# Two transformer blocks on one core: two heads in each attention step, dense groups between the steps

## The reference, cut to what matters

```python
h = rms_norm(x, norm_w);  p = h @ w_in          # split into 18 parts
# A: sparse attention (DSA), 8 heads of 64, indexer of 4 heads
score = einsum('bth,bths->bts', iw, relu(einsum('bthd,bsd->bths', iq, ik)))   # causal
_, sel = top_k(score, 128)
p_a   = softmax(q_cat . kv_cat[sel]);  y_a = (p_a . c_kv[sel]) @ w_uv
# B: stick-breaking attention, 8 heads of 64
z = q k^T / 8;  log_stay = where(strict, log_sigmoid(-z), 0)
a = where(strict, exp(log_sigmoid(z) + cumsum_reverse(log_stay) - log_stay), 0);  y_b = a . v
# C: mLSTM, 4 heads of 128, gates i and f, causal convolution of width 4 + silu on q and k
h_c = num / max(|den|, exp(-m));  y_c = head_layer_norm(h_c) * sigmoid(ml_o)
branches = [y_a * silu(dsa_z), y_b * silu(sb_z), y_c * silu(ml_z)]
mixed = sum_k sigmoid(merge_k) * (branches_k @ w_branch_k);  x = x + mixed @ w_out
```

## Time and profile before

| | us |
|---|---|
| median of three runs | 3041.71 |
| profiled execution | 3063.43 |
| its span | 3061.7 |
| TensorE busy | 2803.4 (92%) |
| VectorE, ScalarE, POOL busy | 1198.1, 1052.6, 1249.1 |
| weight_low on POOL, 398 chunks | 959.1 |
| mean granted clock of TensorE | 0.943 |

### The profile page before, as it was taken

The page is one execution under the profiler, slowest core; times in us unless marked ns, Lnnn a source line. Parts: engine busy times, 40 slices in busy tenths (PEclk is TensorE's granted clock), DMA queues, the critical chain, the costliest instruction groups (busy, mean ns, idle before and its releaser), DMA issues.

```text
span 3061.7 us, 30072 instructions
## 1 busy us (share of the span) xinstructions
PE 2803.4 (92%) x12066; PEld 2149.4 (70%) x12066; DVE 1198.1 (39%) x1739; ACT 1052.6 (34%) x1591; POOL 1249.1 (41%) x803
## 2 busy tenths in 40 slices
PE   7999889989899988998998999997888889899997
PEld 5486667668666766766786887874466768788886
DVE  3652341433347125234323313168885543311112
ACT  3323453432332235443233333241215533332221
POOL 3133343334323333422443443457766334434442
PEclk9799999999989999989999999998788999999999
DMA  3131001122212210111222222231011112222222
GB/s 132 42 108 55 28 28 64 54 76 97 76 62 71 74 43 20 55 55 53 92 96 90 96 97 87 98 125 55 28 35 63 63 48 97 90 87 98 98 97 76
DMA packets 61510, 222.60 MB, mean 73 GB/s; under 512 B 7055, under 2 KB 8591, under 8 KB 60732
## 3 DMA queue, kind: packets, MB, share of 16 engines
q1 hardware_dynamic: 60556, 217.54, 21.0%
q0 software_dynamic: 816, 3.15, 0.3%
HBM read 218.52 MB, written 3.98 MB: 73 GB/s over the span
## 4 chain that ended last, share of the span: by engine, by line
PE 79%; DVE 10%; ACT 6%; POOL 3%; issue 2%; DMA 0%; SPq 0%; DVEq 0%; ACTq 0%
PE proj L154 67%; PE att L681 1%; PE proj L709 1%; DVE hT L432 1%; PE proj L796 1%; PE proj L735 1%; POOL probs L1225 1%; POOL weight_low L132 1%; PE att L726 1%; PE att L755 1%; DVE h_low L426 1%; DVE rstd L429 1%; PE att L700 1%; DVE turned L1115 1%; DVE probs L1137 1%
## 5 line engine op out<-in xcount | busy, mean ns | idle before, releaser
L132 POOL TENSOR_TENSOR weight_low<-ring,weight_high 128x1024 fp32r<-128x1024 f32 x398 | 959.1, 2411 | 1486.7 <-ACT weight_high L124 1486.5
L154 PE MATMUL proj<-h_high,weight_high 128*128 128x512 f32 x2096 | 843.8, 403 | 56.2 <-issue 19.2
L154 PE MATMUL proj<-h_high,weight_low 128*128 128x512 f32 x2096 | 831.8, 397 | 0.0
L154 PE MATMUL proj<-h_low,weight_high 128*128 128x512 f32 x2096 | 830.6, 396 | 0.0
L124 ACT ACTIVATE weight_high<-ring 128x1024 fp32r<-128x1024 f32 x398 | 419.1, 1053 | 488.6 <-PE proj L154 461.5
L154 PEld LDWEIGHTS proj<-h_high,weight_high 128*128 128x128 f32 x2096 | 403.0, 192 | 192.5 <-issue 46.1
L154 PEld LDWEIGHTS proj<-h_low,weight_high 128*128 128x128 f32 x2096 | 403.1, 192 | 87.2
L154 PEld LDWEIGHTS proj<-h_high,weight_low 128*128 128x128 f32 x2096 | 404.3, 193 | 82.1 <-issue 0.2
L2089 DVE TENSOR_TENSOR b_big<-proj,b_big 128x512 f32<-128x512 f32 x44 | 30.4, 691 | 395.6 <-PE proj L154 395.6
L154 PE MATMUL proj<-b_act_high,weight_high 128*128 128x512 f32 x352 | 138.5, 393 | 3.2 <-POOL weight_low L132 3.2
L154 PE MATMUL proj<-b_act_high,weight_low 128*128 128x512 f32 x352 | 138.0, 392 | 0.0
(11 more groups left out here) (391 smaller groups left out, 4211.3 us busy)
## 6 DMA issues: line engine op xcount, KB each, us to landing
ring<-in_stream SPq DMA_DIRECT2D x398, 512.0 KB, 3.2
xT<-in_x SPq DMA_DIRECT2D x2, 1024.0 KB, 6.1
out<-hT SPq DMA_DIRECT2D x1, 2048.0 KB, 6.3
consts<-in_const SPq DMA_DIRECT2D x1, 1088.0 KB, 10.7
bias_rows<-bias_row SPq DMA_DIRECT2D x2, 512.0 KB
b_logits<-in_mem POOLq DMA_DIRECT2D x1, 1024.0 KB, 7.3
bias_rows<-bias_row SPq DMA_DIRECT2D x1, 768.0 KB
raw<-in_wuk SPq DMA_DIRECT2D x2, 256.0 KB, 3.8
```

What stands on the lines that cost most here:

```text
L132: self.s_low.on(pool.tensor_tensor(self.low[:, c % self.slots, :], self.raw[:, c % self.slots, :], self.high[:, c % HIGH, :], ALU.subtract))
L154: mm = pe.matmul(out, a, b, start=(k == 0 and i == 0), stop=(k == n - 1 and i == 2))
```

## The change

In short: (a) Both attentions go through four steps of two heads instead of eight of one. Scores of the two heads alternate, one on array rows 0 to 63, the other on 64 to 127, into banks of their own; the value products alternate on the two column halves into one bank. Transposes and running sums are as many as before, head after head. (b) Dense groups are put between the steps, by the four tables below: the token groups sbv and two groups each of mlq and mlk ahead of the transposes, another behind them, and token groups mlv and all eight gate{d}0 groups around the running sums. The gates are copied out raw, and one sigmoid over 128x4096 is done ahead of the mLSTM heads; mlo and zc stand in those heads instead. Weight chunks come in the new order. (c) The indexer's scores go to attention banks, the largest block of queries first, with ReLU results in four places instead of two. (d) The single matmuls of the rotations, keys, values and gate transposes stand between dense groups, and their results are copied out by ScalarE; the key's and queries' turns, the gate rows and the latent's scaling on VectorE stand inside the 16 rounds of the search. (e) VectorE takes the mean over each head's channels from mv (`centre`), so num comes out centred, and the four mean groups of a layer go. The second head of a pair has soft_high in two tiles of its own.

```diff
+BEFORE_TURN = [[f"sbv{i}" for i in range(4)], [f"sbv{i}" for i in range(4, 8)], ["mlq2", "mlq3"], ["mlk1", "mlk2"]]
+AFTER_TURN = [["mlq0"], ["mlq1"], ["mlk0"], ["mlk3"]]
+BEFORE_SUMS = [[f"mlv{i}" for i in range(4)], ["gate10", "gate20"], [f"mlv{i}" for i in range(4, 8)], ["gate50", "gate60"]]
+AFTER_SUMS = [["gate00"], ["gate30"], ["gate40"], ["gate70"]]
...
+        g += [(n, "a") for n in BEFORE_TURN[p]]
+        g += [(n, "a") for n in AFTER_TURN[p]]
+        g += [(f"dsa{p}", "v")]
+    for p in range(PAIRS_H):
+        g += [(n, "a") for n in BEFORE_SUMS[p] + AFTER_SUMS[p]] + [(f"sb{p}", "v")]
+    g += [("mu0", "a"), ("mm0", "a")]
...
+        def index_scores(part):
+            for b, h in part:
+                r = slice(64 * (h % 2), 64 * (h % 2) + 64)
+                bank, col = (att[4 + h % 2], WQ[1] * (h // 2)) if b == 1 else (att[h], 0)
+                s_sc.on(pe.matmul(bank[:, col:col + WQ[b]], idx[r, h // 2, b * P:(b + 1) * P], idx[r, 2, 0:WQ[b]],
+                                  start=True, stop=True))
...
+        def dsa_scores(p):
+            if p == 0:
+                pe.wait_ge(s_rq.sem, s_rq.base + 4)
+                G.moved(pe, "kk3")
+                pe.wait_ge(s_relu.sem, s_relu.base + 12)
+            else:
+                pe.wait_ge(s_TA.sem, s_TA.base + 2 * p)
+                pe.wait_ge(s_TV.sem, s_TV.base + 4 * p)
+            for b in (3, 2, 0, 1):
                 bank, col = KPLACE[TB - 1 - b]
-                mm = pe.matmul(att[bank][:, col:col + WQ[b]], dq[r, h // 2, b * P:(b + 1) * P],
-                               dk[r, h // 2, 0:WQ[b]], start=True, stop=True)
+                for hh in range(2):
+                    mm = pe.matmul(att[2 * bank + hh][:, col:col + WQ[b]], dq[rows(hh), p, b * P:(b + 1) * P],
+                                   dk[rows(hh), p, 0:WQ[b]], start=True, stop=True)
...
+        def dsa_turn(p):
+            for hh in range(2):
+                pe.wait_ge(s_scaled.sem, s_scaled.base + 8 * p + 4 * (hh + 1))
+                for s in range(TB):
+                    bank, col = KPLACE[s]
+                    for b in range(s, TB):
+                        tr = pe.transpose(att[2 * bank + hh][:, col + (b - s) * P:col + (b - s + 1) * P],
+                                          probs[:, hh, OQ[b] + s * P:OQ[b] + (s + 1) * P], ident)
+                s_T.on(tr)
...
+        def pair_values(name, p, v):
+            out = G.open(pe, name)
+            for s in range(TB):
+                for hh in range(2):
+                    h = 2 * p + hh
+                    mm = pe.matmul(out[rows(hh), s * P:T], v[:, s, h * HD:(h + 1) * HD],
+                                   turned[:, hh, KOFF[s]:KOFF[s] + WK[s]], start=(s == 0), stop=(s == TB - 1),
+                                   skip_group_check=True)
...
+        dsa_scores(0)
+        for p in range(PAIRS_H):
+            fill(BEFORE_TURN[p])
+            dsa_turn(p)
+            fill(AFTER_TURN[p])
+            if p + 1 < PAIRS_H:
+                dsa_scores(p + 1)
+            else:
+                sb_scores(0)
+            dsa_values(p)
+        for p in range(PAIRS_H):
+            fill(BEFORE_SUMS[p])
+            sb_sums(p)
+            fill(AFTER_SUMS[p])
+            if p + 1 < PAIRS_H:
+                sb_scores(p + 1)
+            sb_values(p)
...
+        ml_rows(0)
+        ml_scores(0)
+        ml_scores(1)
+        for h in range(ML_H):
+            dense(f"mlo{h}")
             gated_product(2 * h, 0)
...
+        ml_rows(0)
+        G.moved(act, f"dsa{PAIRS_H - 1}")
+        for j in range(4):
+            s_zh.on(act.activation(z_high[0][:, j, :], za[:, j, :], ACT.Copy))
+        settle(act, s_a)
+        s_gate0.on(act.activation(mixed, mixed, ACT.Sigmoid))
+        for h in range(ML_H):
+            move(f"mlo{h}", mlo[:, h, :], ACT.Sigmoid)
+            W.round(act, f"proj{2 * h}0")
             move(f"den{h}", dn, ACT.Abs)
-            first_gate(2 * h + 1)
-            G.moved(act, f"mean{h}")
+            move(f"zc{h}", zc[:, h, :], ACT.Silu)
+            W.round(act, f"proj{2 * h + 1}0")
+            G.moved(act, f"num{h}")
             s_sq2.on(act.activation(hsq, hml, ACT.Square))
             move(f"var{h}", rstd[:], ACT.Sqrt, scale=1.0 / ML_D, bias=S.eps)
+            if h + 1 < ML_H:
+                ml_rows(h + 1)
         G.whole(act, f"num{ML_H - 1}")
...
+        for i in range(TOPK // 8):
             for b in range(1, TB):
                 x = score[:, OQ[b]:OQ[b] + WQ[b]]
                 link(dve.max(top8[:, b, :], x))
                 link(dve.match_replace(out=x, in_to_replace=top8[:, b, :], in_values=x, imm_value=TAKEN))
+            if i == 1:
+                latent()
+            if i == 4:
+                turn_key()
+            if i == 5:
+                gate_rows()
+            if 9 <= i <= 12:
+                turn_query(i - 9)
...
+            names = BEFORE_TURN[p]
+            for hh in range(2):
+                W.rest(pool, names[-1] if hh else names[len(names) // 2 - 1])
+                pool.wait_ge(s_rinv.sem, s_rinv.base + 2 * p + hh + 1)
+                for b in range(TB):
+                    x = probs[:, hh, OQ[b]:OQ[b] + WQ[b]]
+                    o = 24 + 4 * hh + b
+                    s_scaled.on(pool.tensor_scalar(x, x, small[:, o:o + 1], 1.0, ALU.mult, ALU.mult))
+            W.rest(pool, AFTER_TURN[p][-1])
...
+            names = BEFORE_SUMS[p]
+            softplus(p, 0)
+            fill(names[0:len(names) // 4])
+            softplus(p, 1)
+            fill(names[len(names) // 4:len(names) // 2])
+            softplus_high(p, 0)
+            fill(names[len(names) // 2:3 * len(names) // 4])
+            softplus_high(p, 1)
+            fill(names[3 * len(names) // 4:])
+            sb_exp(p, 0)
+            sb_exp(p, 1)
+            fill(AFTER_SUMS[p])
...
+            names = BEFORE_SUMS[p]
+            W.rest(pool, names[0])
+            for hh in range(2):
+                pool.wait_ge(s_sp.sem, s_sp.base + 3 * (2 * p + hh + 1))
+                for s in range(TB):
+                    s_spm.on(triangle(probs[:, hh, KOFF[s]:KOFF[s] + P], ALU.is_gt, 1, 0.0))
+            W.rest(pool, names[-1])
+            W.rest(pool, AFTER_SUMS[p][-1])
+            for hh in range(2):
+                pool.wait_ge(s_a_exp.sem, s_a_exp.base + 3 * (2 * p + hh + 1))
+                for s in range(TB):
+                    s_am.on(triangle(turned[:, hh, KOFF[s]:KOFF[s] + P], ALU.is_gt, 1, 0.0))
...
+        def centre(i):
+            G.moved(dve, f"mlv{i}")
+            x = mv[:, i % TB, (i // TB) * HALF:(i // TB + 1) * HALF].rearrange("p (a b) -> p a b", a=2)
+            total = small[:, 32 + 2 * i:34 + 2 * i]
+            link(dve.tensor_reduce(total, x, AX.X, ALU.add))
+            s_centred.on(dve.scalar_tensor_tensor(x, total.unsqueeze(2).to_broadcast([P, 2, P]), -1.0 / ML_D, x,
+                                                  ALU.mult, ALU.add))
```

711 lines of the change are left out of this document (353 added, 358 removed).

## The result

| | median us | runs | ratio to before, 95% interval |
|---|---|---|---|
| before | 3043.02 | 4 | 1 |
| after | 2913.48 (2912.25 to 2915.46) | 4 | 0.9557 [0.9532, 0.9582] |

The forecast was 2885, with a range of 2845 to 2948. The kernel became 129.5 us faster, where 156 were forecast. The profiled execution of after took 2912.25 us (span 2910.4), and for that one the sum had said 2907 (span 2906).

The account below looks back on a forecast made before the run. TensorE, busy 2803.4 of 3061.7 us, was taken as the bound. Savings of 23, 24.5, 33.8 and 8.6 made 90 us a layer, 78 after clock loss, 156 in all: 2885 us from the 3041.71 median, range 2845 to 2948.

Parts of the forecast that it names:

- the sum: Stage savings of 90 us a layer, less 12 for clock, 156 in all: span 3061.7 to 2906, execution 2907.
- Packing: Scores and values of both attentions: a pair's 2560 columns take 2.45 us instead of 4.65, 35 us a layer.
- Projections: Stage before the first DSA scores: index scores, rotations, full clock and hand-overs save 23 us a layer, with top-k hidden.
- DSA: DSA stage walked pair by pair: 133.5 us becomes 108 and 1 for switches, 24.5 saved, with waits at second heads' transposes.
- Stick-breaking: Stick-breaking stage with gate groups moved in: 152.2 us becomes 117.4 and 1 for switches, 33.8 saved.
- mLSTM: mLSTM stage: 126.4 us becomes 117.8, saved 8.6; first denominator waits 4.2, gap behind the variance 5.5.
- I take 0.965: TensorE's granted clock in the 345 us behind the projections, 0.93 before; a loss of 12 us a layer.
- The last step: Took the 156 us saving from the median of 3041.71 instead of the profiled execution, giving 2885 us.
- A: The chain sets the step: each pair waits 2.5 us more, mLSTM gaps grow 1 us a head; 2933, chance 0.2.
- B: The clock stays up and waits are half those forecast: 2841 to 2861, chance 0.12.
- C: Packing does nothing, as these matmuls are wider than the second block's: 35 us a layer back, 2955, chance 0.03.
- D: Slower than before: thin fp32 matmuls among dense groups keep TensorE at 1.2 GHz; up to 3335, chance 0.03.

Follow-up runs that it names:

- the serial run: Against after, all matmuls of a pair's first head stand ahead of the second's in scores and values, instead of alternating; 2944.74 us.
- the four extra edits: Against after: POOL's weight chunk behind both scalings, mLSTM scores between broadcast rows, first mLSTM cast ahead of the sigmoid, variance cast behind the exps; 2848.95 us.
- the early cast: Against after, ScalarE casts the weight chunk for mlo0 ahead of z_high and the long sigmoid at the mLSTM walk's start; 2903.04 us.

## Why the prediction came out as it did

A stage's length times its clock is about what it would take at full clock. So the terms can be compared one by one (layer 0, us; the clocks are rounded, so each is good to half a microsecond or so). The product treats a wait as if it too would shrink at full clock, so the last column is the most that the clock can have cost:

| stage | forecast at full clock | measured length x clock | clock loss |
|---|---|---|---|
| projections | 171.2 | 169.7 | 0 |
| DSA | 109 | 110.4 | 3.4 |
| stick-breaking | 118.4 | 120.7 | 0 |
| mLSTM | 117.8 | 113.3 | 14.0 |
| sum | 516.4 | 514.1 | 17.4 (12 forecast) |

**Packing.** Right: 2.43 and 2.38 us for the forecast 2.45. That it comes from alternating the heads, and that most of it lies on the path, the serial run shows.

**Projections.** Right to 1.5 us. The index scores are 4.4 us; the first DSA scores start at 193.21 (196 forecast), and VectorE had been done with the search for 15 us (25 forecast). But most of the 24.5 us saved here are clock, which the sum carries in terms that speak of matmuls: before lost 17.1 us at 0.92 and 0.93, after none. TensorE's idle time in the stage fell with it, from 8.5 us to 1.7.

**DSA.** The walk by the queues named the wait, its releaser and its size: POOL's probs behind a weight_low, 3.3 forecast and 3.16 and 3.15 measured in pairs 0 and 1. In pairs 2 and 3 it was 2.96 and, in two pieces, 4.2, for 2.5. Moving the chunk took it away in pairs 0 and 1 and left 0.63 and, in two pieces, 1.9 in pairs 2 and 3, so the cause is shown.

**Stick-breaking.** 2.3 us over; the waits for soft_low are 14.0 in both layers, and the last values wait 1.33 for POOL (1.8 forecast).

**mLSTM.** The gap behind the variance is 5.5 us, as forecast; the first denominator waits 2.04, not 4.2. This stage alone saved nothing (-0.9 for 8.6), and by the table its clock is the reason: it cost up to 10.2 us before and up to 14.0 after. With the waits taken out the clock is 0.97, and the stage 17.0 us shorter: 9.0 of that is TensorE's idle time and 8.0 its busy time at the same work (116.06 to 108.10).

**The clock.** 17.4 us a layer for 12: the step "I take 0.965" behind the projections was too high, 0.95 was granted. All the same the clock gave more of the gain than a reader of the sum may think: the same stages lost 41 us before (17.1, 3.4, 10.2 and 10.2, from their lengths and granted clocks in the trace), so up to 24 of the 75 saved in a layer are clock, and 51 or more are work and waits. If low clock counts only where TensorE was busy in the two traces, the stages lost 38 us before and 15 after, 23 saved. The sum has such a gain in it (41 less 12, 29 of its 78) and does not name it.

**The last step failed.** 2885 came from taking 156 off the median of 3041.71. But the stages after were built up from prices at full clock; they do not depend on how slow the profiled execution of before was. The sum's own result was the span of 2906, execution 2907, and that was 5 us off. The 22 us between profile and median are clock that one execution had lost, and it lay almost all in the stages that the change rebuilds: the untouched stretches of the two profiles agree within 5 us in sum. I took it off twice. (That the faster executions of before lose 20 us less in just those stages is inferred, since both profiles of before are of its longest executions.) That the sum came within 5 us is luck in part: by the table the mLSTM term came out 4.5 us a layer better than forecast, and the clock 5.4 worse.

**The rivals.** A (every step 2.5 us later) did not come: the waits are those of the walk. B is what the four extra edits made of it, 2849: the clock up and the waits gone. C and D are refuted by the 2.43 us of a pair and the clock of 1.00 in the stick-breaking stage. Not tested by a run of their own are the placing of the single matmuls between dense groups, the gates in the stick-breaking steps and the mean on VectorE; these terms rest on the stage table.

## What to carry to other kernels

Where the stages after are built up from unit prices, compare the sum with the profile it came from and carry only the untouched stretches over from before; do not subtract the saving from another execution's time. Walk each in-order queue past the new order: a 2.4 us weight chunk between two scalings of POOL cost 32 us, and one line moved it. Take out TensorE's waits of 2 to 4 us first, for its clock can fall behind them: 22 us of waits less were 32 us of time.

## What the runs showed of the hardware

- The clock falls behind waits, but not each time. DSA walk of layer 0, waits and work the same, in six profiles: 0.97, 0.91, 0.91, 0.97, 0.94, 0.93. With the heads one after the other, and the transposes' waits 3 us shorter in sum, it was 0.99. With waits of at most 1.6 us it was 1.00, 0.98 and 1.00; with waits up to 7.7 us, 0.88.
- Idle time alone does not do it. The stick-breaking stage of after leaves TensorE idle for 10 of 121 us, in waits of at most 1.7, and the stage had a clock of 1.00 or 0.99 in all eleven profiles of after and its variants; the mLSTM stage with 11 of 127, in waits of 1.3 to 2.0 with 4-row matmuls between them, had 0.89.
- POOL's four masks at the head of the mLSTM stage took 1.03 us in after, where VectorE stood idle, and 2.84 once the early cast had put them beside VectorE's subtraction. The subtraction took 2.50 in after, with POOL idle, and 4.55 beside POOL's weight_low and masks:

```profile
438.34 4.55 DVE L1328 TENSOR_TENSOR z_low<-za,z_high 128x512 fp32r<-128x512 f32 x4 [6.32 <-ACT z_high L1079]
```

```profile
440.21 2.84 POOL L1400 TENSOR_SCALAR_AFFINE_SELECT turned<-turned 128x128 f32<-128x128 f32 x4
```

The Trainium skill (GPSIMD Engine Reference, Specifications) says that POOL shares its SBUF access with VectorE where that reads two tensors; this subtraction does, and the 2.84 against 1.03 agrees, as the earlier trace rows did.
